# Two of the four weight sums of a strip pair formed by accumulating transfers, FFN up-projection of a decoder layer in float32

## The reference, cut to what matters

```python
def conv_ffn(h, w_up, conv_w, conv_b, w_down):
    a, u = jnp.split(h @ w_up, 2, axis=-1)
    a = causal_depthwise_conv(a, conv_w) + conv_b     # width 3 over tokens
    return (jax.nn.silu(a) * u) @ w_down

# one layer: 512 tokens, 1024 features, FFN_DIM 2816, float32
x = x + g1 * dilated_mixture_attention(modulate(x, ...), w_in, w_out)
x = x + g2 * conv_ffn(modulate(x, ...), w_up, conv_w, conv_b, w_down)
return rms_norm(x, norm_final)
```

## Time and profile before

| | us |
|---|---|
| median of 3 runs | 971.48 |
| lowest and highest | 971.14, 971.8 |
| the profiled execution | 971.24 |
| its span, first to last instruction | 969.2 |
| stage of strip pairs 3 to 21, by the timeline | 633.9 to 832.7 |

### The profile page before, as it was taken

How to read it: one execution, slowest core, us unless ns; L and a number is a source line. 1 busy time by engine, 2 the same in 40 slices (tenths; PEclk the granted TensorE clock), 3 DMA queues, 4 the chain that set the end, 5 groups by cost and what they waited for, 6 DMA issues and landing times.

```text
span 969.2 us, 16362 instructions
## 1 busy us (share of the span) xinstructions
PE 943.0 (97%) x5828; PEld 800.2 (83%) x5828; DVE 598.9 (62%) x1304; ACT 447.9 (46%) x804; POOL 19.9 (2%) x39
## 2 busy tenths in 40 slices
PE   7999999999999999999999899999999999999996
PEld 6687887888888888888787788889999999888884
DVE  3445655725737457366473757899999999633325
ACT  7244434436344354363443455655555556523222
POOL 2000000000000000000000001400000000000000
PEclk9999999999999999999999999999999999999999
DMA  9765342433424323344143022433343343532302
GB/s 310 237 199 149 113 127 65 122 118 108 132 62 130 110 91 102 108 124 136 44 131 108 23 58 74 109 88 87 92 125 87 87 124 93 156 105 87 108 1 87
DMA packets 151538, 107.01 MB, mean 110 GB/s; under 512 B 3510, under 2 KB 138830, under 8 KB 151502
## 3 DMA queue, kind: packets, MB, share of 16 engines
q1 hardware_dynamic: 151296, 106.45, 36.6%
q10 hardware_dynamic: 206, 0.08, 0.0%
HBM read 104.42 MB, written 2.10 MB: 110 GB/s over the span
## 4 chain that ended last, share of the span: by engine, by line
PE 73%; DVE 14%; issue 5%; ACT 5%; POOL 1%; DVEq 1%; ACTq 0%; POOLq 0%
PE bank L742 14%; PE bank L744 13%; PE bank L743 13%; DVE wl L1348 4%; PE bank L1002 4%; PE bank L1001 4%; PE bank L1003 4%; PE bank L829 3%; PE bank L805 3%; DVE gate_in L1619 3%; ACT wh L1059 2%; PE bank L769 1%; DVE sums L1653 1%; DVE sums L1650 1%; PE bank L762 1%
## 5 line engine op out<-in xcount | busy, mean ns | idle before, releaser
L1348 DVE TENSOR_TENSOR wl<-raw,wh 128x1024 fp32r<-128x1024 f32 (+1 forms) x127 | 150.1, 1183 | 175.5 <-ACT wh L1059 174.9
L742 PE MATMUL bank<-hh,wl 128*128 128x512 f32 x544 | 221.3, 407 | 0.0
L744 PE MATMUL bank<-hl,wh 128*128 128x512 f32 x544 | 215.4, 396 | 0.0
L743 PE MATMUL bank<-hh,wh 128*128 128x512 f32 x544 | 215.2, 396 | 0.0
L1059 ACT ACTIVATE wh<-raw 128x1024 fp32r<-128x1024 f32 (+1 forms) x127 | 130.1, 1026 | 63.6 <-PE bank L1003 52.2
L742 PEld LDWEIGHTS bank<-hh,wl 128*128 128x128 f32 x544 | 102.7, 189 | 25.8 <-issue 3.5
L744 PEld LDWEIGHTS bank<-hl,wh 128*128 128x128 f32 x544 | 102.4, 188 | 24.4
L743 PEld LDWEIGHTS bank<-hh,wh 128*128 128x128 f32 x544 | 102.6, 189 | 21.5
L952 PE MATMUL bank<-th,wl 128*128 128x256 f32 x304 | 87.4, 287 | 5.2 <-DVE up_late L1687 4.3
L1130 ACT ACTIVATE probs<-probs,nmax 128x256 f32<-128x256 f32 (+1 forms) x128 | 61.9, 485 | 65.8 <-DVE nmax L1424 65.8
L954 PE MATMUL bank<-th,wh 128*128 128x256 f32 x304 | 85.5, 281 | 0.0
(11 more groups left out here) (217 smaller groups left out, 1604.2 us busy)
## 6 DMA issues: line engine op xcount, KB each, us to landing
raw<-in_attn_w_in SPq DMA_DIRECT2D x72, 512.0 KB, 3.8
raw<-in_ffn_w_up SPq DMA_DIRECT2D x34, 512.0 KB, 4.0
ada_raw<-in_w_ada SPq DMA_DIRECT2D x16, 1024.0 KB, 5.9
raw<-in_ffn_w_down SPq DMA_DIRECT2D x17, 512.0 KB, 3.3
raw_up<-in_ffn_w_up SPq DMA_DIRECT2D x10, 512.0 KB, 5.1
ada<-in_w_ada SPq DMA_DIRECT2D x16, 256.0 KB, 6.8
raw<-in_attn_w_out SPq DMA_DIRECT2D x8, 512.0 KB, 4.3
raw_up<-in_ffn_w_down SPq DMA_DIRECT2D x5, 512.0 KB, 3.4
```

What stands on the lines that cost most here:

```text
L742: nc.tensor.matmul(bank[:], wl[:, slot, t], xh[:, t], start=(t == 0), stop=False)
L743: nc.tensor.matmul(bank[:], wh[:, slot, t], xh[:, t], start=False, stop=False)
L744: last = nc.tensor.matmul(bank[:], wh[:, slot, t], xl[:, t], start=False, stop=(t == KT - 1))
L1348: nc.vector.tensor_tensor(dst, src, high.bitcast(F32), ALU.subtract).then_inc(done, 1)
```

## The change

For strip pairs 4 to 21, the sums that don't depend on another sum (0 and 2) are no longer made by VectorE. SP loads the first half of `two` straight into the tiles of sum 0 and sum 2 (`load_sums`, 256 KB each), and GpSimd issues for each a transfer within SBUF that adds its source to what the tile holds (`accum_op=ALU.add`): the second half of `two` onto sum 0, the first half of `one` onto sum 2. VectorE makes sums 1 and 3 as before, after waiting for the transfers (`sum_added`). Since such a transfer only adds, the scheme is rewritten to need sums only: the activation differences change sign, two of the four become three-operand operations with a factor of -1, and so does the product of gate and `u` for pairs 0 to 2; what comes out with the opposite sign is put right at the end by `less_g2`, the negated g2, made once on VectorE. Pair 3 keeps four sums on VectorE (`sum_first`).

`sums` has two sets, one for each parity of f, so that pair f's set can be loaded while pair f-1's is in use: set w is free once the pieces of pair f-2 are split. It fills the room of `h2`; `raw_up` moves behind the other tiles of the stage. The first half of `two` is no longer loaded to `raw`. SP's loop over pairs is written out, and its order per pair is: both loads of sums, each after its wait for pair f-2's low part, then the strip `one` (512 KB), then the second half of `two` (256 KB).

```diff
-        sums = tensor(scope_f, "sums", [P, 4, HK, P])
+        sums = tensor(scope_f, "sums", [P, 8, HK, P])
...
+        def sums_before(f):
+            return 0 if isinstance(f, int) and f == PLAIN else 2 * (f - PLAIN) + 2
+        def sum_uses(f):
+            return f // 2 - 1
...
-            def load_up(f, w):
-                sp.wait_ge(fl_ready, forms_before(f - 1))
-                sp.wait_ge(sums_done, 4 * (f - PLAIN - 1))
-                for u in range(2):
-                    sp.dma_start(up_raw(w)[u], up_columns(f, u)).then_inc(fraw_in[2 * w + u], 16)
-            load_up(5, 1)
-            with sp.Fori(0, (FT - 6) // 2) as m:
-                load_up(2 * m + 6, 0)
-                load_up(2 * m + 7, 1)
+            def load_sums(f):
+                w = f % 2
+                for a in range(2):
+                    if f >= PLAIN + 2:
+                        sp.wait_ge(fl_ready, forms_before(f - 2) + 1 + 2 * a)
+                    sp.dma_start(sums[:, 4 * w + 2 * a], up_columns(f, 1)[:, 0:HK]).then_inc(sum_in[w][a], 16)
+            def load_up(f):
+                w = f % 2
+                sp.wait_ge(fl_ready, forms_before(f - 1))
+                sp.wait_ge(sums_done, sums_before(f - 1))
+                sp.dma_start(up_raw(w)[0], up_columns(f, 0)).then_inc(fraw_in[2 * w], 16)
+                sp.dma_start(up_raw(w)[1][:, HK:KT], up_columns(f, 1)[:, HK:KT]).then_inc(fraw_in[2 * w + 1], 16)
+            for f in range(PLAIN + 1, FT):
+                load_sums(f)
+                if f >= 5:
+                    load_up(f)
...
+            for f in range(PLAIN + 1, FT):
+                w = f % 2
+                one, two = up_raw(w)
+                for a, other_block, came in ((0, two[:, HK:KT], fraw_in[2 * w + 1]), (1, one[:, 0:HK], fraw_in[2 * w])):
+                    pool.wait_ge(sum_in[w][a], 16 * sum_uses(f))
+                    pool.wait_ge(came, loads_of(f, w, None))
+                    nc.gpsimd.dma_start(sums[:, 4 * w + 2 * a], other_block, accum_op=ALU.add).then_inc(sum_added[w][a], 16)
...
+            nc.vector.tensor_scalar(less_g2[:], mod[:, 5 * KT:MOD], -1.0, None, ALU.mult).then_inc(mod_step, 1)
+            dve.wait_ge(mod_step, 2 * len(ADA1) + 3)
...
-                nc.vector.tensor_tensor(tile_of(act_v, f), gate[:], banks[2 * (f % 2) + 1][:], ALU.mult).then_inc(gated, 1)
+                nc.vector.scalar_tensor_tensor(tile_of(act_v, f), gate[:], -1.0, banks[2 * (f % 2) + 1][:], ALU.mult, ALU.mult
+                                               ).then_inc(gated, 1)
...
-            def sum_up(f, w, value):
+            def sum_up(f, w, value, added_value):
-                one, two = up_raw(w)
+                one, at = up_raw(w)[0], 4 * w
                 dve.wait_ge(fraw_in[2 * w], value)
-                dve.wait_ge(fraw_in[2 * w + 1], value)
-                nc.vector.tensor_tensor(sums[:, 0], two[:, 0:HK], two[:, HK:KT], ALU.add).then_inc(sums_done, 1)
-                nc.vector.tensor_tensor(sums[:, 2], one[:, 0:HK], two[:, 0:HK], ALU.subtract).then_inc(sums_done, 1)
-                nc.vector.tensor_tensor(sums[:, 1], sums[:, 0], one[:, 0:HK], ALU.subtract).then_inc(sums_done, 1)
-                nc.vector.tensor_tensor(sums[:, 3], one[:, HK:KT], sums[:, 1], ALU.subtract).then_inc(sums_done, 1)
+                dve.wait_ge(sum_added[w][0], added_value)
+                nc.vector.tensor_tensor(sums[:, at + 1], sums[:, at], one[:, 0:HK], ALU.add).then_inc(sums_done, 1)
+                dve.wait_ge(sums_done, sums_before(f) + 1)
+                dve.wait_ge(sum_added[w][1], added_value)
+                nc.vector.tensor_tensor(sums[:, at + 3], one[:, HK:KT], sums[:, at + 1], ALU.add).then_inc(sums_done, 1)
...
-            nc.vector.tensor_tensor(t32[:, 0], h2[:, 0:HK, HALF:T], h2[:, 0:HK, 0:HALF], ALU.subtract).then_inc(t_done, 1)
+            nc.vector.tensor_tensor(t32[:, 0], h2[:, 0:HK, 0:HALF], h2[:, 0:HK, HALF:T], ALU.subtract).then_inc(t_done, 1)
-            nc.vector.tensor_tensor(t32[:, 1], h2[:, HK:KT, HALF:T], t32[:, 0], ALU.subtract).then_inc(t_done, 1)
+            nc.vector.scalar_tensor_tensor(t32[:, 1], t32[:, 0], -1.0, h2[:, HK:KT, HALF:T], ALU.mult, ALU.subtract
+                                           ).then_inc(t_done, 1)
```

More of the change, by code:

```diff
@@ L112, in decoder_layer @@
         gain = tensor(ctx, "gain", [P, 2, KT])
+        less_g2 = tensor(ctx, "less_g2", [P, KT])
         cond = tensor(ctx, "cond", [P, 5, KT])
@@ L235, in decoder_layer @@
         th_done, tl_done = sem("th_done"), sem("tl_done")
+        sum_in = [[sem(f"sum_in{w}{a}") for a in range(2)] for w in range(2)]
+        sum_added = [[sem(f"sum_added{w}{a}") for a in range(2)] for w in range(2)]
         sums_done, prod_done, copied, added = sem("sums_done"), sem("prod_done"), sem("copied"), sem("added")
@@ L398, in split_last, with split_sums @@
                 split(fh_ready, forms_before(f) + 4, r, wh[:, 3, 0:HK], wl[:, 3, 0:HK], ready)
-        def split_sums(split, f, late, free, ready, dst):
+        def sums_before(f):
+            return 0 if isinstance(f, int) and f == PLAIN else 2 * (f - PLAIN) + 2
+        def sum_uses(f):
+            return f // 2 - 1
+        def split_sums(split, f, w, late, free, ready, dst):
             slot = 1 + late
-            r = sums[:, 2 * late:2 * late + 2].rearrange("p a t n -> p (a t) n")
+            at = 4 * w + 2 * late
+            r = sums[:, at:at + 2].rearrange("p a t n -> p (a t) n")
             if dst is wh:
-                split(sums_done, 4 * (f - PLAIN) + 3 + late, r, wh[:, slot], free, ready)
+                split(sums_done, sums_before(f) + (3 if isinstance(f, int) and f == PLAIN else 1) + late, r, wh[:, slot],
+                      free, ready)
             else:
@@ L450, in loads_next, with adds_next @@
             return loads_of(f + 1, 1 - w, None)
+        def adds_next(f, w, m):
+            if m is not None:
+                return m + 1 if w == 0 else m + 2
+            return sum_uses(f + 1)
         def split_out(split, o, ready, dst):
@@ L1640, in low_form, with sum_first @@
                 nc.vector.tensor_tensor(tl[:, q], t32[:, q], th[:, q].bitcast(F32), ALU.subtract).then_inc(tl_done, 1)
-            def sum_up(f, w, value):
-                one, two = up_raw(w)
-                dve.wait_ge(fraw_in[2 * w], value)
-                dve.wait_ge(fraw_in[2 * w + 1], value)
-                done = 4 * (f - PLAIN)
-                if not (isinstance(f, int) and f == PLAIN):
-                    dve.wait_ge(fl_ready, forms_before(f - 1) + 3)
-                nc.vector.tensor_tensor(sums[:, 0], two[:, 0:HK], two[:, HK:KT], ALU.add).then_inc(sums_done, 1)
-                nc.vector.tensor_tensor(sums[:, 2], one[:, 0:HK], two[:, 0:HK], ALU.subtract).then_inc(sums_done, 1)
-                dve.wait_ge(sums_done, done + 1)
-                nc.vector.tensor_tensor(sums[:, 1], sums[:, 0], one[:, 0:HK], ALU.subtract).then_inc(sums_done, 1)
-                dve.wait_ge(sums_done, done + 3)
-                nc.vector.tensor_tensor(sums[:, 3], one[:, HK:KT], sums[:, 1], ALU.subtract).then_inc(sums_done, 1)
+            def sum_first():
+                one, two = up_raw(1)
+                dve.wait_ge(fraw_in[2], 16)
+                dve.wait_ge(fraw_in[3], 16)
+                nc.vector.tensor_tensor(sums[:, 4], two[:, 0:HK], two[:, HK:KT], ALU.add).then_inc(sums_done, 1)
+                nc.vector.tensor_tensor(sums[:, 6], one[:, 0:HK], two[:, 0:HK], ALU.add).then_inc(sums_done, 1)
+                dve.wait_ge(sums_done, 1)
+                nc.vector.tensor_tensor(sums[:, 5], sums[:, 4], one[:, 0:HK], ALU.add).then_inc(sums_done, 1)
+                dve.wait_ge(sums_done, 3)
+                nc.vector.tensor_tensor(sums[:, 7], one[:, HK:KT], sums[:, 5], ALU.add).then_inc(sums_done, 1)
+            def sum_up(f, w, value, added_value):
+                one, at = up_raw(w)[0], 4 * w
+                dve.wait_ge(fraw_in[2 * w], value)
+                dve.wait_ge(sum_added[w][0], added_value)
[3 more added lines that the diff above has]
+                nc.vector.tensor_tensor(sums[:, at + 3], one[:, HK:KT], sums[:, at + 1], ALU.add).then_inc(sums_done, 1)
             split_plain(split_l, 3, fl_ready, wl)
@@ L1729, in add_ffn @@
                 dve.wait_ge(y_done, o + 1)
-                nc.vector.scalar_tensor_tensor(xT[:, o, tokens], y_bank(o)[:, tokens], mod[:, 5 * KT + o:5 * KT + o + 1],
+                nc.vector.scalar_tensor_tensor(xT[:, o, tokens], y_bank(o)[:, tokens], less_g2[:, o:o + 1],
                                                xT[:, o, tokens], ALU.mult, ALU.add).then_inc(x2_done, 1)
```

32 lines of the change are left out of this document (16 added, 16 removed).

## The result

The changed kernel takes **954.49 us** (median of four runs, 953.21 to 957.36) against 971.31 for the kernel before: a ratio of 0.9834, 95% interval 0.9808 to 0.9860.

What follows compares the result with a forecast made beforehand. TensorE, busy 97% of the span, was taken as the bound: 971.24 us profiled, minus 8.6 for the loop's waits, plus 0.3 at the stage's start, gives 962.9, put at 963.0 us with the median's offset; range 961.5 to 978.

Steps and rivals of the forecast that it cites:

- a change can win only what TensorE loses to waits: Whole kernel: TensorE is busy 97% of the span, so only its waits were counted as possible gain.
- The little tile `less_g2`: Start of the stage: one 8-column operation plus a wait, covered by VectorE idling 0.84 us; otherwise under 0.42 us.
- The loop's 8.6 us: Strip pairs 4 to 19: TensorE's wait for `up_late` disappears, period 10.47 to 9.94 us, 8.6 us less.
- The chain: Strip pair: third sum moves from +5.47 to +4.27 us after product 1; the add writing `up_late` ends about +7.8.
- One sign: Loop: forecast falls if VectorE waits for GpSimd's queue ahead of third or fourth sum and the period exceeds 10 us.
- The transfers' price: GpSimd's adding transfers: 4.5 us each, the median of a 512 KB load, with 2.7 and 6.8 as ends.
- The room: Loop: the first adding transfer has 6.5 us from its operand's landing, the second about one more, before TensorE waits.
- GpSimd beside VectorE: Loop: VectorE operations with two SBUF inputs might delay descriptor writing, up to 1.0 us per transfer; still covered, sum unchanged.
- The stage's start: Start of the up-projection stage: operations becoming three-operand cost 0.07 us each, four ahead of 633.86; 0.3 us more.
- A: Rival, loop: adding transfers late, VectorE's wait for them replaces the one removed; 984 us, chance 0.20.
- B: Rival, loop: part of the gain, first transfer near 6.8 us or another link reaching TensorE; 967 us, chance 0.12.
- C: Rival, loop: VectorE's waiting merely moves, transfer and slack meet at 7.6 us, time stays; 971 us, chance 0.05.

Runs made afterwards that it cites:

- e1: Kernel before the change plus one unused 32-byte tile where the change put `less_g2`, nothing else; 962.46 us, ratio 0.9919.
- e5: Changed kernel with `less_g2` allocated behind all other tiles, so no tile of the kernel before moves by 32 bytes; 963.73 us, ratio 0.9920.
- e2: Changed kernel with one more unused 32-byte tile behind `less_g2`, moving everything behind it 32 bytes further; 961.05 us, ratio 0.9889.
- e3: Changed kernel run once more, with nothing altered; 954.63 us, ratio 0.9840.
- e6: Changed kernel with the strip pairs' streamed tiles 32 bytes further on and all tiles behind `fl` 128 bytes; 952.94 us, ratio 0.9817.
- e7: Changed kernel with 64 bytes of padding behind `less_g2`; 954.73 us, ratio 0.9828.
- e9: As e6, but every tile behind `fl` 256 bytes further on than in the changed kernel instead of 128; 953.39 us, ratio 0.9804.
- e11: Changed kernel with one adding transfer per strip pair instead of two, sum 2 added by VectorE in place; 953.34 us, ratio 0.9813.
- e13: Changed kernel with the single adding transfer of e11 and the tile offsets of e9 together; 950.09 us, ratio 0.9787.
- e4: Changed kernel without GpSimd's adding transfers, VectorE waiting for the plain loads alone, those additions left out; 955.51 us, ratio 0.9840.
- e8: Changed kernel with GpSimd's first transfer of each strip pair made twice, the second after the first has landed; 1002.63 us, ratio 1.0329.

## Why the prediction was wrong in size

**What failed** is the premise that "a change can win only what TensorE loses to waits", and with it the treatment of `less_g2`: "The little tile `less_g2` is one operation on 8 columns plus a wait". It was priced as an instruction, and that price was right, nothing. It was not priced as 32 bytes in front of all other tiles. With it failed the silent term that unchanged code costs what it did: the sum had no entry for the 1632 matmuls of the projections and the 480 of the down-projection, and they gave 8.1 and 3.0 us. The slower step of the strip pairs takes 2.7 back, which leaves 8.4. e1, the shift alone, gives 9.0, and e5, the change without the shift, gives 963.73 for the 963.0 forecast.

**The loop's 8.6 us** were right as a mechanism and are 7.5 in e5: the wait for `up_late` is gone in all pairs but one, and that one, behind a late transfer, costs the 1.1 us that are missing. It is not a stray one. In each of the seven profiles with two transfers per pair (after, e2, e3, e5, e6, e7, e9) TensorE waits for `up_late` in pair 4 or 5, for 0.6 to 1.1 us (3.6 in e2), and but for 0.2 us in the changed kernel's pair 6 not later; with one transfer or none (e11, e13, e4) it does not. Why it is the second or third pair of the stage was not tried. In the changed kernel itself only 5.1 us appear, since the step of "0.1183 us", taken over from before, is 0.1200 at the new distance: 84 x 0.0017 = 0.14 us per pair, 2.7 us over 19 pairs, and the two waits take 0.9. Before the change that slower step was free, because TensorE waited anyway (e1: 198.6 us for 198.4).

**The chain** came out as worked out: third sum +4.24 for +4.27, late add +7.94 for +7.8, ScalarE's wait gone. e11 shows that it is the chain and not VectorE's load that counts. One sign was badly set: a period above 10 us with VectorE waiting for GpSimd's queue was to mean that the forecast falls. Both are seen, and yet the chain came out as worked out: 10.08 is 84 x 0.1200, without a pause.

**The transfers' price**, 4.5 us from the nearest load, measured 4.4. There is luck in it: 4.4 is the middle of two kinds. The first transfers of odd pairs take 3.4 us at the median, and 3.6 is the median where there is one per pair (e11); the others, most of them issued right behind another, take 4.8. The ends of 2.7 and 6.8 held the 3.3 to 5.9 of the first profile, not the 8.1 of e2. The room was used up now and then: one to six of 36 made VectorE wait, nearly always ahead of the fourth sum, by 1.8 us at most in the profiles of the change, by 2.0 in e7 and 2.8 in e2.

**GpSimd beside VectorE**: the earlier trace rows gave up to 1.0 us more per transfer, a rule of the Trainium skill ("SBUF — State Buffer", Who interferes with whom) gave nothing, because descriptor writing should escape. An issue took 0.84 to 0.87 us (the first of all 1.01), or up to 1.20 right behind another one, and none took the 1.7 of the disturbed additions. e8 has such issues beside an idle VectorE to compare (timelines of VectorE and GpSimd):

```profile
667.83 0.41 DVE L1676 TENSOR_TENSOR act_v<-gate,bank 128x256 f32 x1
667.92 0.84 POOL L676 DMA_DIRECT2D sums<-raw_up  x1 [5.20 <-DMA sums<-raw_up]
668.46 1.18 POOL L676 DMA_DIRECT2D sums<-raw  x1
...
776.56 1.22 DVE L1388 TENSOR_TENSOR wl<-sums,wh 128x1024 fp32r<-128x1024 f32 x1
776.73 0.84 POOL L674 DMA_DIRECT2D sums<-raw  x1 [7.04 <-DMA raw<-in_ffn_w_up]
```

Behind 668.24 VectorE stands still, and the issue right behind another takes 1.18 us all the same; the one at 776.73 lies wholly inside an operation with both inputs in SBUF and takes 0.84. So the trace agrees with the rule, and the 1.0 us of the earlier trace rows did not come.

**The stage's start**, +0.3 us: pair 3 starts at 634.3 in e5 where 634.2 was forecast, and the wait of 0.93 us behind ScalarE's copy is still there (0.91 after).

**DMA**: "some 70%" by the bytes was 79%.

**Two slips in the sums**: 16 x 0.53 is 8.5 us and not 8.6, and 962.9 and 0.24 give 963.2 and not 963.0. Neither changes the account.

**The rivals.** A did not come; e8 shows that it was a real danger, and that its price was set too low: loads slow down along with the transfers, and TensorE's pauses cost clock. B and C did not come. None of the cases went below 961.5: the range had no room for an effect outside the stage that was edited. 

**What stays open**: why a distance between two tiles sets the step at all, what lies between the distances tried, whether its period is 256 bytes, why 512 and 256 columns want different ones, and what switches the step of 256 columns between 0.1167 and 0.1178 us at +32. Nothing here looks inside TensorE's reads.

## What to carry to other kernels

A new tile, however small, is two changes: its instructions, and the place of everything allocated behind it. Before a difference is credited to an idea, run the old kernel with the new layout and the new one with the old layout; here that split 17 us into 9 and 8. And before moving a second piece of work off a chain, look whether the first has already made it early: one transfer was enough.

## What the runs showed of the hardware

- The start of the streamed tile relative to the weights' tile changes the matmul step: 0.2270 to 0.2333 us for 512 columns, 0.1167 to 0.1200 for 256, at a granted clock of 1.00. It is alike in every kernel that has a distance of -32 or of 0, and an unused tile of 32 bytes is enough (9 us of 971); at +32 the step of 256 columns has two values, 0.1167 and 0.1178, within one execution.
- An adding transfer of 256 KB within SBUF, issued by GpSimd: 0.84 to 1.20 us to issue, whether VectorE runs an operation with both inputs in SBUF or stands still (e8), and 3.3/4.4/5.9 us to landing (min/median/max) at a DMA share of 0.79, up to 8.1 in e2; 3.3/3.6/5.3 with one per pair at a share of 0.59 (e11).
- With the same 2.6 us of idle in 20 us, TensorE's granted clock sometimes stays at full speed (1.00, the changed kernel's first profile) and sometimes falls for a stretch (0.91 in e3, 0.83 in e9); the out-projection then takes 1.7 and 3.0 us longer.
